# The delta rule's triangular inverse: 128-wide products cut into 64x64 ones

## The reference

```python
kk = jnp.einsum('nbhid,nbhjd->nbhij', kc, kc)
lower = jnp.eye(c, dtype=f32) + beta_c[..., :, None] * kk * dec_strict
rhs = jnp.concatenate([beta_c[..., None] * vc, (beta_c * jnp.exp(gam))[..., None] * kc], axis=-1)
sol = lax.linalg.triangular_solve(lower, rhs, left_side=True, lower=True, unit_diagonal=True)
```

## Time and profile before

| what | value |
|---|---|
| median of three runs | 2256.35 us |
| the profiled execution's own time | 2256.49 us |
| its span, first to last instruction | 2254.5 us |
| TensorE matmul busy | 2219.3 us, 98% |
| VectorE, ScalarE busy | 1464.7 us (65%), 1125.7 us (50%) |
| mean granted TensorE clock | 0.998 |

### The profile page before, as it was taken

How to read it: one execution, slowest core, us unless ns; L and a number is a source line. 1 busy time by engine, 2 the same in 40 slices (tenths; PEclk the granted TensorE clock), 3 DMA queues, 4 the chain that set the end, 5 groups by cost and what they waited for, 6 DMA issues and landing times.

```text
span 2254.5 us, 36641 instructions
## 1 busy us (share of the span) xinstructions
PE 2219.3 (98%) x15888; PEld 2056.2 (91%) x15888; DVE 1464.7 (65%) x1626; ACT 1125.7 (50%) x1441; POOL 54.1 (2%) x46
## 2 busy tenths in 40 slices
PE   8999999999999999999999999999999999999998
PEld 7999998888999999888799999988889999998887
DVE  5777567565768748556687667456658766745664
ACT  4555645454455564444464535444446553544443
POOL 0000000000000000000000100000000010000000
PEclk9999999999999999999999999999999999999999
DMA  7545455565655454556555434455655544545653
GB/s 230 181 134 173 140 211 168 185 201 179 186 168 155 155 192 160 180 189 225 157 138 147 131 115 167 161 164 188 206 173 153 146 125 124 168 135 168 202 196 112
DMA packets 296806, 376.97 MB, mean 167 GB/s; under 512 B 22335, under 2 KB 256901, under 8 KB 296646
## 3 DMA queue, kind: packets, MB, share of 16 engines
q1 hardware_dynamic: 296646, 374.62, 52.7%
HBM read 368.10 MB, written 1.05 MB: 164 GB/s over the span
## 4 chain that ended last, share of the span: by engine, by line
PE 91%; DVE 6%; ACT 2%; issue 1%; DMA 0%; SPq 0%; POOL 0%; DVEq 0%; POOLq 0%; ACTq 0%
PE ps L607 17%; PE ps L2223 14%; PE ps L2780 7%; PE ps L617 5%; PE ps L2244 5%; PE ps L2234 4%; PE ps L995 4%; PE ps L904 4%; PE ps L2302 4%; PE ps L619 3%; PE ps L2246 2%; PE ps L673 2%; PE ps L631 2%; PE ps L2291 2%; PE ps L939 2%; PE ps L920 1%
## 5 line engine op out<-in xcount | busy, mean ns | idle before, releaser
L1288 DVE TENSOR_TENSOR a_wlo<-a_ring,a_whi 128x2048 fp32r<-128x2048 f32 (+1 forms) x173 | 393.0, 2274 | 99.2 <-ACT a_whi L1021 98.6
L3112 DVE TENSOR_TENSOR b_wlo<-b_ring,b_whi 128x2048 fp32r<-128x2048 f32 (+1 forms) x168 | 379.5, 2262 | 109.4 <-ACT b_whi L2805 109.2
L1021 ACT CAST a_whi<-a_ring 128x2048 fp32r<-128x2048 f32 (+1 forms) x173 | 328.2, 1899 | 130.2 <-PE ps L904 48.7
L607 PE MATMUL ps<-a_nsp,a_whi 128*128 128x256 f32 x2144 | 387.3, 283 | 0.0
L2805 ACT CAST b_whi<-b_ring 128x2048 fp32r<-128x2048 f32 (+1 forms) x168 | 317.2, 1889 | 125.3 <-PE ps L2780 79.0
L607 PEld LDWEIGHTS ps<-a_nsp,a_whi 128*128 128x128 f32 x2144 | 334.1, 192 | 0.0
L607 PE MATMUL ps<-a_nsp,a_wlo 128*128 128x256 f32 x1072 | 306.3, 286 | 0.0
L2223 PE MATMUL ps<-b_nsp,b_whi 128*128 128x256 f32 x1568 | 284.8, 283 | 0.0
L2223 PEld LDWEIGHTS ps<-b_nsp,b_whi 128*128 128x128 f32 x1568 | 244.0, 191 | 0.1
L2223 PE MATMUL ps<-b_nsp,b_wlo 128*128 128x256 f32 x784 | 228.0, 291 | 4.0 <-ACT b_gates L2860 3.1
L607 PEld LDWEIGHTS ps<-a_nsp,a_wlo 128*128 128x128 f32 x1072 | 205.5, 192 | 1.5 <-issue 1.0
(11 more groups left out here) (572 smaller groups left out, 4400.4 us busy)
## 6 DMA issues: line engine op xcount, KB each, us to landing
b_ring<-in_w_in SPq DMA_DIRECT2D x50, 1024.0 KB, 5.8
a_ring<-in_w_in SPq DMA_DIRECT2D x49, 1024.0 KB, 5.4
a_ring<-in_w_ffn_in SPq DMA_DIRECT2D x44, 1024.0 KB, 5.1
a_ring<-in_w_gate SPq DMA_DIRECT2D x32, 1024.0 KB, 5.4
b_ring<-in_w_up SPq DMA_DIRECT2D x32, 1024.0 KB, 5.4
b_ring<-in_w_down SPq DMA_DIRECT2D x32, 1024.0 KB, 5.0
a_ring<-in_w_ffn_out SPq DMA_DIRECT2D x22, 1024.0 KB, 5.0
a_ring<-in_w_branch SPq DMA_DIRECT2D x16, 1024.0 KB, 5.1
```

The lines of the kernel that those rows point to most:

```text
L607: mm = T.matmul(out, w[:, k, c:c + P], x_[:, k, :], start=k == 0 and n == 0, stop=k == KD - 1 and n == 2)
L1021: nc.scalar.copy(part(whi, h), part(ring, h)).then_inc(hi_ok, 1)
L1288: nc.vector.tensor_tensor(part(wlo, h), part(ring, h), part(whi, h).bitcast(F32), ALU.subtract).then_inc(lo_ok, 1)
L3112: nc.vector.tensor_tensor(part(wlo, h), part(ring, h), part(whi, h).bitcast(F32), ALU.subtract).then_inc(lo_ok, 1)
```

## The change

The last level, block 64, is the only one that couples the two 64-column halves of a system. Up to it, X, XT and LT are block diagonal. The change keeps only the diagonal blocks: LTm, XTd, X, LTd and Y are 128 x 8 x 64 tiles, with the upper left block of a system on partitions 0 to 63 and the lower right one on 64 to 127.

- A product of two 128x128 block-diagonal matrices becomes two of 64x64. At level 1 and in `first_inverse` the two sit on the two diagonal quarters of TensorE's array and write one bank. At levels 2 to 5 the order BLOCKS goes over all four quarters; the two row halves write different banks (2 and 3, or 4 and 6).
- `first_inverse` and the turn at level 6 are now matmuls with the identity instead of transposes. At levels 2 to 5 one transpose of 128x128 turns the blocks of two systems, 4 instead of 8.
- Level 6 multiplies only the lower left block: 8 products of 64x64 on one quarter for Y, 8 for Z, and one negation into XT.
- The two halves of four systems are gone: one Y copy, one XT copy (two at level 6), one subtraction per level, one semaphore count each.
- `lower()` has a memset and seven multiplications or subtractions of 64x512 instead of one of 128x1024 and four of 128x512. The mask of level 6 is gone.

The core of the diff (left out: the semaphore totals in `GAINED_2`, the new offsets of the tiles, the single waits on the other engines):

```diff
+    DIAG = [(slice(64 * q, 64 * q + 64), slice(64 * q, 64 * q + 64)) for q in range(2)]
+    LOW, HIGH = slice(0, 64), slice(64, P)
+    BLOCKS = [(2 * p + s, q) for p in range(4) for s, q in ((0, 0), (1, 1), (1, 0), (0, 1))]
...
+        def of(bank_, n):
+            return ps[:, bank_, n * 64:(n + 1) * 64]
...
         def first_inverse():
-                for s in range(4 * p, 4 * p + 4):
-                    mm = T.transpose(ps[:, 2 + p, (s % 4) * P:(s % 4 + 1) * P], XT[:, s, :], ident)
-                mm.then_inc(x0_ps, 1)
+            for s in range(8):
+                for r, c in DIAG:
+                    mm = T.matmul(of(2, s)[r], XTd[r, s, :], ident[r, c], start=True, stop=True)
+            mm.then_inc(x0_ps, 1)
...
         def solve_y(lv):
-                for s in range(4 * p, 4 * p + 4):
-                    mm = T.matmul(ps[:, 2 + p, (s % 4) * P:(s % 4 + 1) * P], LTm[:, s, :], X[:, s, :],
-                                  start=True, stop=True)
+            if lv < 6:
+                pe.wait_ge(lm_ok, lv)
+                for s, q in BLOCKS:
+                    r, bank_ = DIAG[q][0], 2 + (q if lv > 1 else 0)
+                    to, n = (DIAG[s % 2][0], s // 2) if lv > 1 else (r, s)
+                    mm = T.matmul(of(bank_, n)[to], LTm[r, s, :], X[r, s, :], start=True, stop=True)
+            else:
+                for s in range(8):
+                    mm = T.matmul(of(2, s)[HIGH], LT[LOW, s, HIGH], X[LOW, s, :], start=True, stop=True)
...
         def solve_z(lv):
+                for s, q in BLOCKS:
+                    to = DIAG[q][0]
+                    if lv == 1:
+                        out, xt, y_ = of(4, s)[to], XTd[to, s, :], Y[to, s, :]
                     else:
+                        r = DIAG[s % 2][0]
+                        out, xt, y_ = of(4 + 2 * (s % 2), s // 2)[to], XTd[r, s // 2 * 2 + q, :], Y[r, 4 * q + s // 2, :]
+                    mm = T.matmul(out, xt, y_, start=True, stop=True)
+            else:
+                for s in range(8):
+                    mm = T.matmul(of(4, s)[LOW], Y[HIGH, s, :], XT[HIGH, s, HIGH], start=True, stop=True)
...
         def inverse_turn(lv):
+            if lv < 6:
+                for p in range(4):
+                    mm = T.transpose(ps[:, 5, p * P:(p + 1) * P], flat(X[:, 2 * p:2 * p + 2, :]), ident)
+            else:
+                for s in range(8):
+                    for r, c in DIAG:
+                        mm = T.matmul(of(5, s)[r], X[r, s, :], ident[r, c], start=True, stop=True)
...
         def lower():
-            link(V.tensor_tensor(LT[:, :, :], LT[:, :, :], row_pair[0], ALU.mult))
+            V.memset(XT[HIGH, :, LOW], 0.0)
+            for r, c in DIAG:
+                V.tensor_tensor(LTd[r, :, :], LT[r, :, c], row_pair[0][r, :, c], ALU.mult)
+            link(V.tensor_tensor(LT[LOW, :, HIGH], LT[LOW, :, HIGH], row_pair[0][LOW, :, HIGH], ALU.mult))
...
         def inverse(lv):
+            else:
+                ins = V.tensor_scalar(XT[LOW, :, HIGH], z[LOW], -1.0, None, ALU.mult)
```

More of the change, by code:

```diff
@@ L158 @@
     "sgw_ps": 1, "few_ps": 1, "ct_ps": 1, "up_q": 1, "cum_ps": 1, "l2_ps": 1, "qk_ps": 2, "pt_ps": 5, "o_ps": 5,
-    "mix_ps": 1, "sa_ps": 9, "turn_ps": 6, "go_ps": 1, "dec_ps": 1, "tk_ps": 1, "kk_ps": 1, "x0_ps": 12,
-    "yy_ps": 12, "zz_ps": 12, "u_ps": 2, "st_ps": 1, "ks_ps": 1, "do_ps": 1, "out_used": 6, "res_ps": 6,
+    "mix_ps": 1, "sa_ps": 9, "turn_ps": 6, "go_ps": 1, "dec_ps": 1, "tk_ps": 1, "kk_ps": 1, "x0_ps": 6,
+    "yy_ps": 6, "zz_ps": 6, "u_ps": 2, "st_ps": 1, "ks_ps": 1, "do_ps": 1, "out_used": 6, "res_ps": 6,
     "wk_ps": 4, "qv_ps": 8, "xs_ps": 4, "up_ps": 16, "dn_used": 15, "hi_ok": 84, "in_ms": 4, "nhi_ok": 24,
@@ L167 @@
     "ln_ok": 1, "mx_ok": 6, "pt_v": 1, "lev_ok": 2, "o_ok": 1, "mix_ok": 2, "sa_ok": 9, "free_v": 3, "l2_ok": 1,
[L168 removed]
+    "go_ok": 1, "hn_ok": 2, "tk_ok": 1, "lt_ok": 1, "xx_ok": 7, "at_ok": 1, "lm_ok": 5, "pr_free": 16,
     "mg_ok": 12, "u_ok": 2, "st_ok": 2, "yl_ok": 1, "ml_ok": 4, "x_ok": 6, "xpn_ok": 4, "ol_ok": 4, "hs_ok": 14,
@@ L1842, in second_block @@
     gv, gog = at("gv", [P, NT, W2], offset=base + 20480), at("gog", [P, NT, W2], offset=base + 22528)
-    decT, LT, LTm, X, XT, Y = (at(n, [P, 8, P], offset=base + 4096 * i)
-                               for i, n in enumerate(("decT", "LT", "LTm", "X", "XT", "Y")))
+    decT, LT, XT = (at(n, [P, 8, P], offset=base + 4096 * i) for i, n in ((0, "decT"), (1, "LT"), (4, "XT")))
+    LTm, XTd, X, LTd, Y = (at(n, [P, 8, 64], offset=base + 2048 * i)
+                           for i, n in ((4, "LTm"), (5, "XTd"), (6, "X"), (7, "LTd"), (10, "Y")))
+    DIAG = [(slice(64 * q, 64 * q + 64), slice(64 * q, 64 * q + 64)) for q in range(2)]
+    LOW, HIGH = slice(0, 64), slice(64, P)
+    BLOCKS = [(2 * p + s, q) for p in range(4) for s, q in ((0, 0), (1, 1), (1, 0), (0, 1))]
     attnT = decT
@@ L2488, in key_products @@
             mm.then_inc(kk_ps, 1)
+        def of(bank_, n):
+            return ps[:, bank_, n * 64:(n + 1) * 64]
         def first_inverse():
             pe.wait_ge(tk_ok, 1)
-            for p in range(2):
-                pe.wait_ge(xx_ok, p + 1)
-                for s in range(4 * p, 4 * p + 4):
-                    mm = T.transpose(ps[:, 2 + p, (s % 4) * P:(s % 4 + 1) * P], XT[:, s, :], ident)
-                mm.then_inc(x0_ps, 1)
-        def solve_y(lv):
[L2499 to L2504, removed]
-                for s in range(4 * p, 4 * p + 4):
-                    mm = T.matmul(ps[:, 2 + p, (s % 4) * P:(s % 4 + 1) * P], LTm[:, s, :], X[:, s, :],
-                                  start=True, stop=True)
-                mm.then_inc(yy_ps, 1)
@@ L2510, in solve_z @@
-        def solve_z(lv):
[L2511 to L2521, removed]
-                    else:
-                        mm = T.matmul(ps[:, 5 + 2 * p, c], Y[:, s, :], XT[:, s, :], start=True, stop=True)
-                mm.then_inc(zz_ps, 1)
@@ L2526, in inverse_turn @@
-        def inverse_turn(lv):
[L2527 to L2531, removed]
+            pe.wait_ge(xx_ok, 1)
+            for s in range(8):
+                for r, c in DIAG:
+                    mm = T.matmul(of(2, s)[r], XTd[r, s, :], ident[r, c], start=True, stop=True)
@@ new lines, in first_inverse @@
+            mm.then_inc(x0_ps, 1)
+        def solve_y(lv):
+            pe.wait_ge(xx_ok, lv)
+            if lv == 1:
+                pe.wait_ge(x0_ok, 1)
+            if lv < 6:
[7 more added lines that the diff above has]
+                    mm = T.matmul(of(2, s)[HIGH], LT[LOW, s, HIGH], X[LOW, s, :], start=True, stop=True)
+            mm.then_inc(yy_ps, 1)
@@ new lines, in solve_z @@
+        def solve_z(lv):
+            pe.wait_ge(yy_ok, lv)
+            if lv == 1:
+                pe.wait_ge(at_ok, 1)
+            else:
+                pe.wait_ge(x0_ok, lv)
+            if lv < 6:
+                for s, q in BLOCKS:
+                    to = DIAG[q][0]
+                    if lv == 1:
+                        out, xt, y_ = of(4, s)[to], XTd[to, s, :], Y[to, s, :]
+                    else:
+                        r = DIAG[s % 2][0]
[4 more added lines that the diff above has]
+                    mm = T.matmul(of(4, s)[LOW], Y[HIGH, s, :], XT[HIGH, s, HIGH], start=True, stop=True)
+            mm.then_inc(zz_ps, 1)
@@ L2533, in solution @@
+        def inverse_turn(lv):
+            pe.wait_ge(xx_ok, lv)
+            if lv < 6:
+                for p in range(4):
[4 more added lines that the diff above has]
+                        mm = T.matmul(of(5, s)[r], X[r, s, :], ident[r, c], start=True, stop=True)
+            mm.then_inc(x0_ps, 1)
         def solution(t):
-            pe.wait_ge(*((xx_ok, 14), (st_ok, 2))[t])
+            pe.wait_ge(*((xx_ok, 7), (st_ok, 2))[t])
@@ L2896, in inverse_out @@
         def inverse_out():
-            for p in range(2):
-                act.wait_ge(x0_ps, p + 1)
-                A.copy(flat(X[:, 4 * p:4 * p + 4, :]), ps[:, 2 + p, :]).then_inc(x0_ok, 1)
+            act.wait_ge(x0_ps, 1)
+            A.copy(flat(X), ps[:, 2, :]).then_inc(x0_ok, 1)
         def inverse_turned(lv):
-            for p in range(2):
-                act.wait_ge(x0_ps, 2 * (lv - 1) + p + 1)
-                A.copy(flat(XT[:, 4 * p:4 * p + 4, :]), ps[:, 5 + 2 * p, :]).then_inc(x0_ok, 1)
-        def y_out(lv):
[L2907 to L2912, removed]
+            act.wait_ge(x0_ps, lv)
+            if lv < 6:
+                A.copy(flat(XTd), ps[:, 5, :]).then_inc(x0_ok, 1)
+                return
+            for r, c in DIAG:
+                ins = A.copy(XT[r, :, c], ps[r, 5, :].rearrange("p (s i) -> p s i", s=8))
+            ins.then_inc(x0_ok, 1)
+        def y_out(lv):
+            act.wait_ge(yy_ps, lv)
+            if lv >= 2:
+                act.wait_ge(zz_ps, lv - 1)
+            r = slice(0, P) if lv < 6 else HIGH
+            src = ps[r, 2:4, 0:4 * 64] if 1 < lv < 6 else ps[r, 2, :].rearrange("p (q c) -> p q c", q=2)
```

(35 more changed lines are left out.)

2 lines of the change are left out of this document (1 added, 1 removed).

## The result

The changed kernel takes 2233.14 us, the median of four runs (2232.08 to 2233.70); the kernel before took 2256.34 in the same session (four runs). The ratio is 0.9899, 95% interval 0.9887 to 0.9911: 1.0% faster, 23.2 us. The forecast was 2234.0 with a range of 2230.5 to 2243. The profiled execution's span fell from 2254.5 to 2231.7 us.

What follows compares the result with a forecast made beforehand. PE was taken as the bound, busy 98% of the span. Its bursts fall from 26.58 to 15.44 us a layer, 22.3 us for two layers: 2256.49 to 2234.2, less 0.14 for the median, 2234.0 us; range 2230.5 to 2243.

Steps and rivals of the forecast that it cites:

- What bounds the kernel: Whole span: PE is busy for 98% and is 91% of the chain, so time lost by PE's bursts shortens the end.
- The price of a burst: PE's small bursts: 0.34 us once for leaving and re-entering the full array, plus 0.058 us a round.
- Four quarters at once: Levels 2 to 5: four quarters work together, 8 rounds a burst, 64 rounds a layer; the forecast, with no bank rule, 45%.
- rival 1: Levels 2 to 5: only two quarters work at once, 128 rounds instead of 64, +7.4, 2241.4 us; chance 20%.
- rival 2: `first_inverse`, level 1, level 6's turn: row halves writing the same bank take turns, +7.4, 2241.4 us; chance 9%.
- rival 3: Bursts of levels 2 to 5: records issue 0.026 us apart, not 0.0145, +5.9, 2239.9 us; chance 10%.
- the two readings of the 25 ns: Skill's start-to-start floor for small matmuls: per record it gives rival 3's time, per product it changes nothing.
- rival 4: All small bursts: 64x64 quarters don't overlap, 416 rounds a layer instead of 160, +29.7, 2263.9 us; chance 4%.
- Level 6: Y, its turn and Z take 16 rounds each, 48 together; Y under its turn would save 1.9 us.
- The other engines at nothing: Copies, subtractions, `lower()`, end of the levels and DMA: each covered by PE's work, so costed at nothing.
- my list of covers: Work hiding other engines' steps, such as 2.87 us of fills over the Y and X copies.
- `lower()`: VectorE before `first_inverse`: about 5.0 us instead of 4.0, done at 1260.9, tightest cover at 0.6 us.

Runs made afterwards that it cites:

- the doubled rounds: The changed kernel with every product of Y and Z at levels 2 to 5 issued twice: 2240.16 us.
- the split burst: The changed kernel with two of the four transposes at levels 2 to 5 moved into the middle of Y's burst: 2234.72 us.

## Why the prediction was right, point by point

- **What bounds the kernel.** Right. The chain still names PE for 91%, and the sum of the bursts, 22.4 us, is the span's 22.8 but for 0.4; merging the halves alone gave 1.0002.
- **The price of a burst, 0.34 plus 0.058 a round.** Right, taken from a burst of another shape. 16 rounds cost 1.27 and 8 rounds 0.82, which gives 0.056 to 0.058 a round and 0.34 to 0.37 of edges; the doubled rounds and the split burst changed one of the two each and moved by 0.47 and 0.31. The Trainium skill ("TensorEngine Tiling (Array Packing)", Key Properties) says that changing the tiling mode drains the engine. The 0.31 is a price of that kind; the trace doesn't show what the engine does in it.
- **Four quarters at once (against rival 1).** Right, and the largest open term. Four records begin within 0.04 us. It took two rows that each showed half of it, and the earlier trace rows for four at once.
- **Row halves in one bank (rival 2).** Did not happen: level 1's Y writes bank 2 from both row halves and begins a pair every 0.058. The Trainium skill ("TensorEngine Tiling (Array Packing)", Restrictions and Gotchas) says that different row tiles cannot access the same PSUM bank at the same time. In this kernel, where the two write different partitions of the bank, the trace shows no turns being taken. Row halves on the same partitions of one bank were not tried.
- **The issue of records (rival 3).** Did not happen, also not in a row of 64: a record every 0.0145 us, a product every 0.029. Of the two readings of the 25 ns in the prediction, the one per record is out; the one per product stands.
- **The slow side (rival 4).** Did not happen; but the run in another order shows how near it lies: with products quarter by quarter, the Z bursts of levels 2 to 5 cost 1.66, hardly less than the 1.78 of the 128-wide ones.
- **Level 6.** Mis-sized by 0.18 a layer: Y and the turn overlapped in the last three of Y's rounds. I had named an overlap as a chance, and a full one of 16 rounds, not as the forecast. The turn's first records begin when 13 of Y's 16 are out:

```profile
1308.43 0.97 PE L2518 MATMUL ps<-b_X,b_LT 64*64 64x64 f32 x13
1309.18 0.27 PE L2549 MATMUL ps<-con,b_X 64*64 64x64 f32 x2
```

- **The other engines at nothing.** The step that failed, in size: a bank's release was not on my list of covers. I had covered the copies that the levels themselves need, but not ScalarE's emptying of the fill's bank behind block 21, which a burst of 1.78 covered and one of 0.82 does not: 0.25 us a layer. Level 6's 0.18 and the turns' 0.16 the other way made the sum come out at 15.42 for 15.44. The bursts of Y with their turns are at 1.20 what 0.31 of edges instead of 0.34 would give; why they are cheaper there no run shows.
- **The number.** That 2234.0 lies within 0.9 us of 2233.14 is partly luck. The price of a burst is shown, but the sum agrees to 0.02 because terms that are wrong by a third of a microsecond each way cancel, and the 23.2 us between the medians are 22.4 of bursts and 0.8 of spread.
- **`lower()`.** Held, more narrowly than forecast. VectorE's timeline:

```profile
1255.69 0.48 DVE L3410 MEMSET b_XT<- 64x512 f32 x1 [2.60 <-issue]
...
1259.72 1.39 DVE L3418 TENSOR_TENSOR b_XTd<-con,b_XTd 64x512 f32<-64x512 f32 x2
```

It ends at 1261.11 after 5.4 us, not 5.0, because two operations on different partition halves take 1.39 where two of 128x512 took 1.28. PE's first record there begins at 1261.33: 0.2 us of cover left where I had counted 0.6.

## What to carry to other kernels

Price a burst of small products by its edges and its rounds, read from any burst in the trace that uses part of the array: here 0.34 us plus 0.058 us a round of 64 float32 columns, however many quarters work in it. Then go round all quarters in the order of the program, one product each, and don't split a burst: one more trip out of the full array cost 0.31 us. When a burst gets shorter, list everything that waited under it, the release of the next fill's bank as well as the burst's own copies.

## What the runs showed of the hardware that I had not expected

- Leaving the full array and returning costs much the same in the middle of float32 products (0.31 us) as between the fills (0.34 to 0.37), with 8 rounds or with 16.
- Program order decides the overlap: with four products in a row on one quarter, the next quarter's work begins about three records early and no more (22.8 rounds in place of 8).
- ScalarE's copies and VectorE's subtractions read one partition half of a bank and write the other at no extra cost that shows: two of each four cross over and two don't, and all of ScalarE's take 0.35 to 0.37 us, all of VectorE's 0.41 to 0.43. Cutting into 64x256 does cost: four copies take 1.5 us and four subtractions 1.7, beside 0.59 and 0.69 for one of 128x512.
